# Root of the norm behind router and expert products, a sixth expert buffer, and another order of routing, in a mixture-of-experts decoder step on one Trainium2 core

## What is computed

```python
x = x + (jax.nn.sigmoid(ga) * y_a + jax.nn.sigmoid(gb) * y_b) @ w_out
x = x + hier_moe(rmsnorm(x, g_ffn), w_rg, b_rg, w_re, b_re, w_gate, w_up, w_down)

# rmsnorm: r = rsqrt(mean(x*x) + eps); (x * r) * g
# hier_moe, t = the normed rows:
g_logits = t @ w_rg + b_rg                       # 4 groups: the best one is taken
e_logits = t @ w_re + b_re                       # 8 experts of that group: the best two
hid = silu(t @ w_gate[e]) * (t @ w_up[e])        # 32 experts, 1024 -> 256
out = sum over the two chosen e of combine[e] * (hid @ w_down[e])   # 256 -> 1024
```

## Time and profile before

| | us |
|---|---|
| median of 3 runs | 1280.32 |
| lowest, highest | 1277.23, 1281.22 |
| profiled execution | 1276.03 |
| its span, first to last instruction | 1274.3 |
| TensorE busy in it | 1159.6 |
| VectorE, ScalarE, GpSimd busy | 638.8, 251.0, 295.3 |

### The profile page before, as it was taken

The page is one execution under the profiler, slowest core; times in us unless marked ns, Lnnn a source line. Parts: engine busy times, 40 slices in busy tenths (PEclk is TensorE's granted clock), DMA queues, the critical chain, the costliest instruction groups (busy, mean ns, idle before and its releaser), DMA issues. The chain is left out here.

```text
span 1274.3 us, 15342 instructions
## 1 busy us (share of the span) xinstructions
PE 1159.6 (91%) x5791; PEld 829.5 (65%) x5791; DVE 638.8 (50%) x1266; ACT 251.0 (20%) x470; POOL 295.3 (23%) x245
## 2 busy tenths in 40 slices
PE   4999998889999989999999998997799987888896
PEld 3887886678788866688888886454455444443342
DVE  6356687545367875555545445256233323222565
ACT  3232220002322100153111000111122212112122
POOL 2304130122223111134444442011222211221000
PEclk9999998999999888899999999997699989999899
DMA  6222211231321123622222244405499999997301
GB/s 214 67 66 67 67 50 54 85 97 55 99 66 34 50 71 103 205 70 67 97 69 93 73 154 140 207 34 199 155 379 388 373 396 388 402 389 287 138 33 38
DMA packets 95138, 191.82 MB, mean 151 GB/s; under 512 B 9126, under 2 KB 72438, under 8 KB 82776
## 3 DMA queue, kind: packets, MB, share of 16 engines
q1 hardware_dynamic: 89364, 181.73, 39.5%
q0 software_dynamic: 5440, 8.94, 2.2%
q10 hardware_dynamic: 260, 0.16, 0.0%
HBM read 180.68 MB, written 17.98 MB: 156 GB/s over the span
## 5 line engine op out<-in xcount | busy, mean ns | idle before, releaser
L1066 PE MATMUL ps<-arena,weights 128*128 128x272 f32 x2240 | 538.6, 401 | 0.7 <-DVE arena L789 0.7
L1066 PEld LDWEIGHTS ps<-arena,weights 128*128 128x128 f32 x2240 | 429.4, 194 | 95.3 <-issue 6.9
L571 POOL TENSOR_TENSOR weights<-weights 128x512 f32<-128x512 f32 x160 | 219.6, 1382 | 552.5 <-PE ps L1066 496.2
L1563 PE MATMUL ps<-arena 128*64 128x256 f32 x832 | 106.1, 413 | 22.0 <-DMA arena<-in_w_up 21.8
L1563 PEld LDWEIGHTS ps<-arena 128*64 128x64 f32 x832 | 62.3, 148 | 56.7 <-DMA arena<-in_w_up 23.9
L1650 DVE TENSOR_SCALAR arena<-arena 64x256 f32<-64x256 f32 x32 | 9.1, 285 | 154.2 <-ACT arena L1614 154.2
L615 ACT ACTIVATE arena<-ps 128x272 f32<-128x272 f32 x80 | 31.4, 393 | 250.7 <-PE ps L1066 250.7
L1523 POOL DMA_INDIRECT expert_rows<-arena x32 | 29.2, 914 | 195.5 <-DVE arena L1665 188.4
L1242 PE MATMUL ps<-weights,arena 128*128 128x512 f32 (+1 forms) x160 | 69.2, 636 | 4.2 <-PEq L476 4.2
L750 DVE TENSOR_TENSOR arena<-arena 128x272 f32<-128x272 f32 x40 | 41.2, 1029 | 58.6 <-ACT arena L615 57.8
L1821 PE MATMUL ps<-arena 128*128 128x512 f32 (+1 forms) x160 | 64.7, 606 | 1.4 <-DVE arena L1890 1.4
(11 more groups left out here) (238 smaller groups left out, 1253.3 us busy)
## 6 DMA issues: line engine op xcount, KB each, us to landing
weights<-in_w_in SPq DMA_DIRECT2D x36, 1024.0 KB, 5.1
arena<-in_w_gate SPq DMA_DIRECT2D x26, 1024.0 KB
arena<-in_w_up SPq DMA_DIRECT2D x26, 1024.0 KB
arena<-in_w_down SPq DMA_DIRECT2D x26, 1024.0 KB
weights<-in_w_gate SPq DMA_DIRECT2D x6, 1024.0 KB
weights<-in_w_up SPq DMA_DIRECT2D x6, 1024.0 KB
weights<-in_w_down SPq DMA_DIRECT2D x6, 1024.0 KB
arena<-in_x_prompt SPq DMA_DIRECT2D x8, 512.0 KB, 6.1
```

What stands on the lines that cost most here:

```text
L571: nc.gpsimd.tensor_tensor(SW[:, i], x, y, op).then_inc(s_ready, 1)
L1066: ins = mm(ps[:, b, 0:HF], w4[:, k, :], x4[:, k, :], start=(k == 0), stop=(k == 3))
L1563: ins = mm(ps[u * UP:u * UP + CAP, 2 + s, 0:DE], xgT[s][:, k, :], w[e % 5][:, k, :], start=(k == 0), stop=(k == KT - 1))
```

## The change

- `g_ffn` no longer scales rows. The router weights are multiplied by it once (`gffn` by column, in the order of `x1`), and for the experts it is applied when the turned rows are copied out of PSUM (`gperm`), now by VectorE alone.
- The root of the norm is applied behind the products: to the logits in `choose`, and for the experts through the table, which gets a fourth column (`vl`, `rec`, `RV`, `tb`, `half_rt`). The scaling L1386 is gone, and `x1` itself is stored for the gather (`x1_dram`), in natural order; so `turn` reads `xg[s][0:CAP, k:D:KT]`, every eighth word.
- All transposes of the expert block use 64 rows; the zeroing of `hid` is gone. The results `yo` stand in partitions 64 to 127 of `xg`.
- Six expert buffers; experts 1 to 3 are loaded at the start of the routing block, 4 and 5 when the products with `w_out` are done. `g_final` is loaded late in the expert block.
- Tiles are taken in the order 4, 0, 1, 2, 3 (`ORDER`). The table sums of the first three tiles come before the last product, the fourth before the last rank.

The overflow block follows suit and isn't shown.

```diff
-        eb = [area(EB[i], 6144) for i in (2, 1, 3, 0)] + [W_flat[:, 0:6144]]
-        wg = [b[:, 0:2048].rearrange("p (k n) -> p k n", k=KT) for b in eb]
-        wu = [b[:, 2048:4096].rearrange("p (k n) -> p k n", k=KT) for b in eb]
-        wdn = [b[:, 4096:6144].rearrange("p (k n) -> p k n", k=2) for b in eb]
+        N = (R["m@"] + 1792, R["m@"] + 3840, R["tmp@"] - 960)
+        parts = [[area(at + 2048 * i, 2048) for i in range(3)] for at in (EB[2], EB[1], EB[3])] + [[area(at, 2048) for at in N]]
+        parts += [[area(EB[0] + 2048 * i, 2048) for i in range(3)], [W_flat[:, 2048 * i:2048 * i + 2048] for i in range(3)]]
+        wg, wu = ([b[i].rearrange("p (k n) -> p k n", k=KT) for b in parts] for i in range(2))
+        wdn = [b[2].rearrange("p (k n) -> p k n", k=2) for b in parts]
...
+                            sp.dma_start(gffn, a["g_ffn"].rearrange("o (k p) -> p (o k)", p=P)).then_inc(r_loaded, 16)
+                            sp.dma_start(gperm, a["g_ffn"].rearrange("o (p k) -> p (o k)", k=KT)).then_inc(r_loaded, 16)
...
-                for e in (1, 2):
+                for e in (1, 2, 3):
                     load_gate_up(sp, e)
                     load_down(sp, e)
-                for t in range(NT):
-                    if t == NT - 1:
-                        sp.wait_ge(wo_ready, NT)
-                        load_gate_up(sp, 3)
-                        load_down(sp, 3)
-                        sp.dma_start(wpp, a["w_ple_proj"][0].rearrange("(k p) n -> p k n", p=P)).then_inc(pp_loaded, 16)
-                    sp.wait_ge(h2_ready, t + 1)
-                    sp.dma_start(h2_dram[tok(t), :], h2[t % 2][0:TOK[t], :]).then_inc(h2_out[t % 2], 16)
-                load_gate_up(sp, 4)
-                load_down(sp, 4)
-                sp.dma_start(gfin, a["g_final"].unsqueeze(0).to_broadcast([P, D])).then_inc(gf_loaded, 16)
-
-                sp.wait_ge(h2_out[0], 48)
-                sp.wait_ge(h2_out[1], 32)
+                for i, t in enumerate(ORDER):
+                    sp.wait_ge(x1_ready, i + 1)
+                    sp.dma_start(x1_dram[tok(t), :], x1[0:TOK[t], t, :]).then_inc(x1_out, 16)
+                sp.wait_ge(wo_ready, NT)
+                for e in (4, 5):
+                    load_gate_up(sp, e)
+                    load_down(sp, e)
+                sp.dma_start(wpp, a["w_ple_proj"][0].rearrange("(k p) n -> p k n", p=P)).then_inc(pp_loaded, 16)
+
+                sp.wait_ge(x1_out, 16 * NT)
...
+                def route(i):
+
+                    t, n = ORDER[i], TOK[ORDER[i]]
+                    pe.wait_ge(x1_ready, i + 1)
+                    if i:
+                        pe.wait_ge(h2t_copied, i)
                     for k in range(KT):
-                        ins = tr(ps[:, 4 + k // 4, (k % 4) * P:(k % 4) * P + n], h2[t % 2][0:n, k * P:k * P + P], ident[0:n, 0:n])
+                        ins = tr(ps[:, 4 + k // 4, (k % 4) * P:(k % 4) * P + n], x1[0:n, t, k * P:k * P + P], ident[0:n, 0:n])
...
+                pe.wait_ge(wo_loaded[0], 16)
+                project(1, (0,))
+                pe.wait_ge(wo_loaded[1], 16)
+                project(0, (0, 1))
+                project(1, (1,))
                 route(0)
-                for t in range(NT):
-                    if 0 < t < NT - 2:
-                        project(t + 1, (1,))
-                        rank(t)
-                    if t + 2 < NT:
-                        project(t + 2, (0,) if t + 2 < NT - 1 else (0, 1))
-                    if t in (0, NT - 2, NT - 1):
-                        rank(t)
-                    if t + 1 < NT:
-                        route(t + 1)
-                    if t == NT - 2:
-                        for u in range(NT - 1):
-                            table(u)
-                            total(u)
-
-                table(NT - 1).then_inc(table_sum, 1)
-                total(NT - 1).then_inc(rank_ready, 1)
+                project(2, (0,))
+                rank(0)
+                route(1)
+                project(2, (1,))
+                rank(1)
+                project(3, (0,))
+                route(2)
+                project(3, (1,))
+                rank(2)
+                project(4, (0,))
+                route(3)
+                for i in range(3):
+                    table(i)
+                    total(i)
+                project(4, (1,))
+                rank(3)
+                route(4)
+                before_rank(4)
+                table(3)
+                total(3)
+                own_rank(4)
+                table(4).then_inc(table_sum, 1)
+                total(4).then_inc(rank_ready, 1)
...
+                v.tensor_tensor(wr, wr, gffn.unsqueeze(2).to_broadcast([P, KT, 36]), ALU.mult).then_inc(wr_ready, 1)
...
-                    v.scalar_tensor_tensor(h2[t % 2][0:n, :].rearrange("p (k q) -> p q k", k=KT),
-                                           x1[0:n, t, :].rearrange("p (q k) -> p q k", k=KT), rs[0:n, t:t + 1],
-                                           gffn[0:n, :].rearrange("p (q k) -> p q k", k=KT), ALU.mult,
...
-                    link(v.tensor_tensor(L, ps[0:n, 6, 0:36], rb[0:n, :], ALU.add))
+                    link(v.scalar_tensor_tensor(L, ps[0:n, 6, 0:36], rs[0:n, t:t + 1], rb[0:n, :], ALU.mult, ALU.add))
...
+                for i in range(2):
+                    residual(i)
+                    root(i)
+                for i in range(NT):
+                    choose(i)
+                    if 0 < i < NT - 1:
+                        residual(i + 1)
+                    place(i)
+                    if 0 < i < NT - 1:
+                        root(i + 1)
...
-                for e in range(NE - 5):
+                for e in range(NE - 6):
                     sp.wait_ge(gu_ready, e + 1)
-                    load_gate_up(sp, e + 5)
+                    load_gate_up(sp, e + 6)
                     if e:
                         sp.wait_ge(dn_ready, e)
-                        load_down(sp, e + 4)
-                sp.wait_ge(dn_ready, NE - 5)
+                        load_down(sp, e + 5)
+                sp.wait_ge(dn_ready, NE - 6)
                 load_down(sp, NE - 1)
                 for c in range(2):
-                    sp.wait_ge(dn_ready, NE - 4 + c)
+                    sp.wait_ge(dn_ready, NE - 5 + 2 * c)
+                    if c:
+                        sp.dma_start(gfin, a["g_final"].unsqueeze(0).to_broadcast([P, D])).then_inc(gf_loaded, 16)
...
-                for i in range(2):
-                    nc.gpsimd.memset(hid[i], 0.0).then_inc(hid_zero, 1)
...
-                        r = CAP if k else P
-                        ins = tr(ps[:, k // 4, (k % 4) * P:(k % 4) * P + r], xg[s][0:r, k * P:k * P + P], ident[0:r, 0:r])
+                        ins = tr(ps[:, k // 4, (k % 4) * P:(k % 4) * P + CAP], xg[s][0:CAP, k:D:KT], ident[0:CAP, 0:CAP])
...
-                        r = CAP if k else P
-                        ins = tr(ps[:, 6, k * P:k * P + r], hid[e % 2][0:r, k:DE:2], ident[0:r, 0:r])
+                        ins = tr(ps[:, 6, k * P:k * P + CAP], hid[e % 2][0:CAP, k:DE:2], ident[0:CAP, 0:CAP])
...
-                    nc.scalar.activation(sg[s][0:CAP], ps[0:CAP, 2 + s, 0:DE], ACT.Tanh, scale=0.5).then_inc(tanh_done, 1)
-                    nc.scalar.activation(up[s][0:CAP], ps[UP:UP + CAP, 2 + s, 0:DE], ACT.Copy).then_inc(up_copied, 1)
+                    nc.scalar.activation(sg[s][0:CAP], ps[0:CAP, 2 + s, 0:DE], ACT.Tanh,
+                                         scale=half_rt[0:CAP, e:e + 1]).then_inc(tanh_done, 1)
+                    nc.scalar.activation(up[s][0:CAP], ps[UP:UP + CAP, 2 + s, 0:DE], ACT.Copy,
+                                         scale=tb[0:CAP, e:e + 1, 3].bitcast(F32)).then_inc(up_copied, 1)
...
-                    v.tensor_copy(xgT[s][:, 4:8, :], ps[:, 1, :].rearrange("p (k t) -> p k t", k=4)[:, :, 0:CAP]).then_inc(t_cp_v, 1)
+
+                    v.tensor_tensor(xgT[s], ps[:, 0:2, :].rearrange("p s (k t) -> p (s k) t", k=4)[:, :, 0:CAP],
+                                    gperm.unsqueeze(2).to_broadcast([P, KT, CAP]), ALU.mult).then_inc(t_copied, 1)
```

285 lines of the change are left out of this document (131 added, 154 removed).

## The result

The changed kernel takes 1266.41 us, the median of 4 runs (1259.63 to 1268.30), where the kernel before took 1278.78 (4 runs, 1274.73 to 1281.22). The ratio is 0.9897, with a 95% interval from 0.985 to 0.9943: faster by 12.4 us or 1.0%. In three later comparisons with more runs each, an unchanged copy of the changed kernel stood at 0.9939, and at 0.9927, and a copy of the kernel before at 1.0001. So some 7 to 9 us are what repeats, and the first comparison shows rather more. The forecast was 5.3 us faster, 1275.0, with a range of 1266 to 1283. The sign held and the range held by 0.4 us; the size was too small, by more than half against the first comparison and by some 2 to 3 us against what repeats.

The account below looks back on a forecast made before the run. Weight loads bound the expert stage. Routing 5.0 us earlier, loop start +3.3, then TensorE's 248.8 us instead of 252.7, with g_final's 0.3, gave 5.3 us faster: median 1275.0 us, range 1266 to 1283.

Parts of the forecast that it names:

- edit 3: Expert loop, turn reading every eighth word: +0.158 us a load, 1.26 us an expert on TensorE.
- edit 1: Expert stage, sixth buffer: one expert fewer in the load stream, 252.7 - 8.9 = 243.8 us; late g_final costs 0.3.
- What bounds the kernel before: Expert stage: weight loads set the pace at 8.89 us an expert; TensorE has 2.0 us of slack per expert.
- Edit 2: Norm's root behind products; gain applied in VectorE's 512-column copy, 0.69 us, +0.28, hidden in steady loop, +0.5 at start.
- The term for the 64 rows: Expert loop, both kinds of turn using 64 partitions throughout: -0.25 us an expert, from 0 to -0.4.
- The sum: Expert loop: TensorE's 248.8 us exceeds the loads' 243.8; gate_up(31) 5.6 us earlier, 5.3 with g_final; median 1275.0.
- Rival B: Expert loop: stride eight costs what two costs, period about 7.1, loads set the pace; 1269.9 us, chance 0.26.
- Edit 4: Routing, short tile first: last product 4.7 us later, 13.6 to 15.3 us behind it, flag 5.0 us earlier.
- rival D: Routing hardly shorter as TensorE falls to 1.2 GHz, flag 898.5; gather waits full 3 us; 1279.5 us, chance 0.15.
- Start of the loop: First gather behind queued expert loads +1.5 us (0 to 3), removed memsets -0.6; gate_up(0) at 907.1 instead of 908.8.
- The two strided turns in the open: Before the first expert products, two strided turns at half clock: +1.9 us.
- Rival C: Expert loop: strided load above +0.185 us, period past 8.10; slower, mostly 1282 to 1295, up to 1330; chance 0.14.

Follow-up runs that it names:

- a shorter period (6.49): Changed kernel with each turn reading 128 words in a row instead of every eighth word: 1267.30 us, ratio 0.9941 to the kernel before.
- a longer one (7.76): Changed kernel with each turn's eight transposes done twice: 1268.46 us, ratio 0.9941 to the kernel before.
- the sweep: Changed kernel plus a block behind the last stage, 16 transposes at each of seven word distances from 1 to 31: 1297.87 us in one execution.
- a nominal 8.64: Changed kernel with each turn's transposes done three times: 1313.36 us in one execution.

## Why the prediction was right and where it was wrong

The step that failed is the size of edit 3's term, and with it the claim that TensorE is what comes late next. The sign came from edit 1, whose term was right.

**What bounds the kernel before: right.** The loads set the pace then, at 8.9 us an expert, and in the changed kernel they still do: the waits for w_up remain, and neither a shorter period (6.49) nor a longer one (7.76) moved the median by more than 1.2 us, with intervals of some 2 to 3 us to either side.

**Edit 1, six buffers: right.** The term was 252.7 - 8.9 = 243.8 us. Measured are 242.0 to 245.5, 243.4 in the mean, and 250.3 with five buffers. The last stage is as long as it was (112.8 and 111.5 before, 111.6 to 111.9 after), so `g_final` cost nothing that shows, where I had 0.3.

**Edit 2, the copy with the gain: right.** It takes 675 ns in the median, for which I had 0.69 us, and the period of 6.88 shows that it is hidden in the loop.

**Edit 3, the stride: here the size failed.** I took one doubling between two ends, +0.158 us a load and 1.26 us an expert. It costs 0.38 us an expert, below even the 0.44 that was the lower bound. The reason that I gave, that the growth from one to two has no reason to stop at once, is refuted by the sweep: it stops at two. The row nearest in kind was the strided load of L1587, 193 ns; I set it below a supposition about growth and an analogy with VectorE. The line rule that I had cited from the Trainium skill (Advanced Engine Details and Errata, SBUF Cachelines) foresees the penalty at distances 4 and beyond, where a line of 16 bytes gives one word. It doesn't fit distance 2: a line still gives two words there, and the load is already at its full price.

The term for the 64 rows was mis-sized the other way, -0.25 us an expert where -0.38 came: 0.19 in each kind of turn. The two errors together put TensorE's period at 7.89 instead of 6.88.

**The sum: wrong by that step.** "What is late next is TensorE" isn't so. TensorE's side of the sum, 3.4 + 31 x 6.88 = 216.7 us, is far below the loads' 243.8. Rival B had named this, with a stride of eight at the price of two, loads setting the pace and gate_up(31) 10.7 us earlier, 10.4 with `g_final`. Counted from the first product, gate_up(31) moved from +368.9 and +368.0 to +360.1, +359.8 and +359.3, 8.7 us. B's 1269.9 us, with its difference of -10.4, is the nearest of the cases to what was measured.

**Edit 4, the order of routing: right in the first profile, less so in the others.** Counted from the first product, the last product was to end 4.7 us later and did so by 5.2 (875.58 - 792.65 = 82.9, and 883.07 - 794.96 = 88.1). Behind it I had 13.6 to 15.3 us, and 14.3 came. The flag was to come 5.0 us earlier, and came 5.5 earlier. But the two other profiles of the same kernel show it only 1.8 and 2.4 us earlier, since their last product ended at +92.1 and +91.3. All eleven profiles with this order of routing fall into two groups: the flag at +102.4 to +103.2 in five, near the forecast's +102.9, and at +105.5 to +106.2 in six, near the +105.9 of rival D. The windows from 865 to 890 us show that the clock differs, the changed kernel first, then its copy:

```profile
865.00:890.00 25.00, 22.58 (x102) 14.54 (x100) 9.18 (x46) 3.88 (x7) 2.87 (x3) 0.89 0.19 68
```

```profile
865.00:890.00 25.00, 22.79 (x82) 13.66 (x80) 6.94 (x33) 3.72 (x7) 1.45 (x2) 0.80 0.05 18
```

And here is the first early table sum with what follows it, again in the two:

```profile
871.62 0.65 PE L1285 MATMUL ps<-arena 32*64 32x128 f32 x4
...
874.27 8.80 PE L1240 MATMUL ps<-weights,arena 128*128 128x512 f32 x16
```

```profile
872.72 1.11 PE L1285 MATMUL ps<-arena 32*64 32x128 f32 x4
...
877.43 9.27 PE L1240 MATMUL ps<-weights,arena 128*128 128x512 f32 x16
```

The three tables and totals took 2.65 us in one execution and 4.71 in the other, at full and at half clock: 0.65 and 1.11 for the same four products. That is 2.1 of the 3.9 us by which the last product ended later in the copy. I had costed them at full clock alone, 2.1 us, and even there they took 2.65. Rival D had named a fall of the clock, and both its halves came: up to 3.7 us of the flag's gain, and the gather below.

**Start of the loop: the gather was mis-sized.** I took +1.5 us, with 3 as the end; it was 7.4 - 3.0 = +4.4, and +3.2 to +3.4 in the other traces of this kernel, all outside the bounds. The scatters' 6.7 us from issue to landing were the row to go by: a gather behind queued loads lands after 7.9 in the median. The source view of the gathers in the changed kernel:

```profile
DMA to landing us min/median/max: 2.9/7.9/8.8
```

The zeroing of `hid` that was removed gave nothing: the gather was issued 1.8 us behind the flag in both kernels (900.51 to 902.36, 897.33 to 899.14). The two strided turns in the open, for which I had 1.9 us, cost nothing either: from the first turn to gate_up(0) it took 3.06 us, where it was 3.40. In the first profile gate_up(0) came 1.5 us earlier, where I had 1.7, but that is luck: the gather was 2.9 us dearer than its term, and the turns, copies and memsets together 2.1 us cheaper, the flag half a microsecond better. In the other traces it came from 1.8 us earlier to 1.6 us later.

**Rival C: rightly unlikely.** Its condition, a load of over +0.185, was far from what was measured, and the crossing it named, a period of 8.10 us, is in line with both neighbours tried: no loss to speak of at 7.76, and a loss of 43 us in the loop at a nominal 8.64. Of these 43 its price explains 28 (to 271.2); that the clock falls too it left out.

**What stays open.** The first comparison gave 12.4 us and the later ones 7.1 and 8.7. The stages of the three copies explain 8.7, up to gate_up(31), and the sweep's trace has it another 3 to 4 us earlier without a cause that I could name. For the other 3.7 of the first comparison I have none either, and the spread of single runs (1259.63 to 1268.30) is larger than that. How the gain divides between the sixth buffer and the routing is shown by the times only, not by the one trace with five buffers.

## What to carry to other kernels

When two limits are close, the forecast is decided by the one term that would carry one past the other, so that term deserves the row nearest in kind, and not a rule of growth laid through two points. A shorter period on the engine that isn't the bound, or an earlier start of it at the expense of the transfers, showed nothing in the time; one more buffer, filled in a stretch in which the DMA engines had been nearly idle, was worth 7.9 us of time. And a small indirect transfer that is sent behind megabytes of queued loads has to be charged with the landing time that such transfers show under load elsewhere in the same trace.

## What the runs showed of the hardware

- A weight load of 128 words in each of 64 partitions takes 139 ns and follows the last after 0.062 us when the words stand in a row, at a granted clock of 1.00. At distances from 2 to 16 words it took 0.11 to 0.12 us from start to start, at a granted clock of 0.50 as well as of 1.00. At 0.50 eight transposes took 1.15 us strided and 1.11 contiguous, so the stride's price is gone there.
- One transpose of 128 rows ahead of seven of 64 made the turn of the gathered rows 0.19 us longer, and one ahead of one did the same to that of the hidden rows.
- A gather of 64 rows took 3.0 us from issue to the turn that reads it with the DMA engines nearly idle, and 6.2 to 7.4 behind the queued loads of two experts and `w_ple_proj`.
- TensorE ran without a gap at a granted clock of 1.00 in one kernel (period 7.76 us) and of 0.89 in another (8.65 to 10.01), with the DMA engines busy in both (1.01 and 1.00). In the second the clock fell to 0.50 for about 3 us behind 24 transposes in a row, in some periods and not in others.
